# The weight block that the last product reads is cut last, and what was queued around it is reordered

## What is computed

```
uv = jax.nn.gelu(h @ w_in, approximate=False)          # stage 0: layer 0, gated mixer
u, v = jnp.split(uv, 2, axis=-1)
v = _rmsnorm(v, v_norm_g)
z = jnp.einsum("gts,bnsgc->bntgc", w_causal, v) + b_s.T[None, None, :, :, None]
y = (u * z) @ w_out
...
y = jnp.square(jax.nn.relu(h @ mlp_w_up[layer])) @ mlp_w_down[layer]   # stages 1 and 2: layers 0 and 1
```

## Time and profile before

| | |
|---|---|
| median of 3 runs | 2595.98 us (2595.35 to 2597.56) |
| the profiled execution's own time | 2595.35 us |
| span from its first to its last instruction | 2593.3 us |
| PE busy in the span | 2523.0 us (97%) |
| DVE busy | 1581.6 us (61%) |
| ACT busy | 988.1 us (38%) |
| mean granted clock of TensorE, of full speed | 0.991 |

### The profile page before, as it was taken

How to read it: one execution, slowest core, us unless ns; L and a number is a source line. 1 busy time by engine, 2 the same in 40 slices (tenths; PEclk the granted TensorE clock), 3 DMA queues, 4 the chain that set the end, 5 groups by cost and what they waited for, 6 DMA issues and landing times.

```text
span 2593.3 us, 33660 instructions
## 1 busy us (share of the span) xinstructions
PE 2523.0 (97%) x12220; PEld 2061.2 (79%) x12220; DVE 1581.6 (61%) x1907; ACT 988.1 (38%) x1423; POOL 149.0 (6%) x151
## 2 busy tenths in 40 slices
PE   6999999999999999999999997999999999999999
PEld 4888888888888878888898886666788888888887
DVE  6878766668867656675723624777258565544442
ACT  5543342236454421111302323777326445311110
POOL 0000000000000000000000003666000000000000
PEclk9999999999999999999999997999999999999999
DMA  6335573213444475553142353564322332632311
GB/s 253 126 134 182 192 265 106 98 57 146 166 151 151 174 276 176 204 186 114 51 157 91 113 173 99 114 137 105 123 114 94 110 117 109 251 122 82 112 47 68
DMA packets 122980, 359.60 MB, mean 139 GB/s; under 512 B 12032, under 2 KB 28416, under 8 KB 118912
## 3 DMA queue, kind: packets, MB, share of 16 engines
q1 hardware_dynamic: 122880, 358.23, 41.0%
HBM read 270.10 MB, written 88.08 MB: 138 GB/s over the span
## 4 chain that ended last, share of the span: by engine, by line
PE 84%; DVE 7%; DMA 3%; ACT 3%; issue 1%; SPq 0%; DVEq 0%; ACTq 0%
PE PS L2034 24%; PE PS L2036 24%; PE PS L2035 24%; DVE KEEP L1954 2%; DMA MODRAW<-in_modw 2%; PE PS L2514 2%; PE PS L2501 2%; PE PS L2482 1%; ACT PS L1269 1%; PE PS L2138 1%; PE PS L2140 1%; PE PS L2139 1%; PE PS L2438 1%; PE PS L2483 1%; DVE T_RAW L1553 1%
## 5 line engine op out<-in xcount | busy, mean ns | idle before, releaser
L2034 PE MATMUL PS<-HID_HI,W_HI 128*128 128x512 f32 x1024 | 400.1, 391 | 5.8 <-DVE HID_LO L1604 5.0
L2035 PE MATMUL PS<-HID_LO,W_HI 128*128 128x512 f32 x1024 | 398.5, 389 | 0.0
L2036 PE MATMUL PS<-HID_HI,W_LO 128*128 128x512 f32 x1024 | 398.5, 389 | 0.0
L374 ACT ACTIVATE W_HI<-RAW 128x1024 fp32r<-128x1024 f32 x114 | 119.5, 1059 | 615.5 <-PE PS L2036 510.2
L1450 DVE SCALAR_TENSOR_TENSOR X<-PS,MODV,X 128x1024 f32<-128x1024 f32 x124 | 159.0, 1282 | 284.2 <-PE PS L2036 275.6
L2034 PE MATMUL PS<-H_HI,W_HI 128*128 128x512 f32 x700 | 277.5, 396 | 3.7 <-DVE H_LO L1394 2.6
L2036 PE MATMUL PS<-H_HI,W_LO 128*128 128x512 f32 x700 | 273.5, 391 | 0.0
L2035 PE MATMUL PS<-H_LO,W_HI 128*128 128x512 f32 x700 | 273.3, 390 | 0.0
L2034 PEld LDWEIGHTS PS<-HID_HI,W_HI 128*128 128x128 f32 x1024 | 192.2, 188 | 50.4 <-DVE HID_LO L1604 7.9
L2036 PEld LDWEIGHTS PS<-HID_HI,W_LO 128*128 128x128 f32 x1024 | 192.2, 188 | 40.0
L2035 PEld LDWEIGHTS PS<-HID_LO,W_HI 128*128 128x128 f32 x1024 | 192.3, 188 | 39.5 <-issue 0.2
(11 more groups left out here) (223 smaller groups left out, 4922.7 us busy)
## 6 DMA issues: line engine op xcount, KB each, us to landing
RAW<-in_wt SPq DMA_DIRECT2D x208, 512.0 KB, 4.0
MODRAW<-in_modw SPq DMA_DIRECT2D x96, 512.0 KB, 3.5
HRAW<-hid_scratch SPq DMA_DIRECT2D x14, 2048.0 KB, 9.5
hid_scratch<-TN SPq DMA_DIRECT2D x90, 256.0 KB, 2.2
hid_scratch<-SCR SPq DMA_DIRECT2D x84, 256.0 KB, 2.2
x_scratch<-X SPq DMA_DIRECT2D x3, 4096.0 KB, 13.9
X<-x_scratch SPq DMA_DIRECT2D x6, 2048.0 KB, 9.0
QK<-qk_scratch SPq DMA_DIRECT2D x16, 768.0 KB, 6.3
```

The source lines that it names most:

```text
L374: act.activation(ring_view(W_HI, n), raw_view(n), ACT.Copy).then_inc(sem["w_hi"], 1)
L2034: pe.matmul(dst, w_hi, m_hi, start=first, stop=False)
L2035: pe.matmul(dst, w_hi, m_lo, start=False, stop=False)
L2036: return pe.matmul(dst, w_lo, m_hi, start=False, stop=last)
```

## The change

A22 becomes the last block that is cut, on ACT and on DVE, in every pair; since `load_pair` still waits for it, the load of the next pair's weights moves behind it too. In SP's queue `load_pair` now stands behind `store(p, 0, 0, 0, 0)` and one or two `load_mod`. `first_pair` begins with `c11`, and cuts the five blocks behind `c21`; in pair 1 (`second`) `c11` stands first. `WS_RAW` moves from the place of MODRAW to the place of WY_HI and WY_LO and is loaded after the last product of pair 12. TensorE's program is not edited.

```diff
--- before.py
+++ after.py
@@ -29,7 +29,7 @@
 PAIRS = UPS // 2 - 2
 PRODUCTS = 7
 BLOCKS = 6
-A1, A22, S2, S1, S3, S4 = range(BLOCKS)
+A1, S2, S1, S3, S4, A22 = range(BLOCKS)
 RELU_AT = {2: 1, 5: 2, 6: 3, 7: 4}
 VPAIRS = 6
 VHALF = [0, 1, 1, 0]
@@ -287,7 +287,7 @@
 
         V_TOT = at("V_TOT", [P, 2, HALF], F32, RX + 28 * KB)
         V_IN = at("V_IN", [P, 2, 2, HALF], F32, RX + 16 * KB)
-        WS_RAW = at("WS_RAW", [P, GROUPS, CHUNK], F32, RC)
+        WS_RAW = at("WS_RAW", [P, GROUPS, CHUNK], F32, RX + 24 * KB)
         W_RAW1 = at("W_RAW1", [P, 8, RING * P], F32, RR)
         R_RAW0 = at("R_RAW0", [P, 4, HALF], F32, RB)
         PO2 = at("PO2", [P, 2, HALF], F32, RB + 48 * KB)
@@ -535,10 +535,10 @@
                         sp.dma_start(RAW[:, f, :], wt[(p * 2 + t0 + 6 + f).v]).then_inc(sem[f"raw_in{f}"], 16)
 
                 def pair(p, x):
-                    load_pair(p + 1)
                     store(p, 0, 0, 0, 0)
                     if mods:
                         load_mod(sp, p // 2 * 3 + GMODS + 1 + 2 * x)
+                    load_pair(p + 1)
                     if mods and x == 0:
                         load_mod(sp, p // 2 * 3 + GMODS + 2)
                     store(p, 2, 0, 1, 1)
@@ -616,22 +616,22 @@
                     store(p, None, 1, 3, 1)
 
                 def v_pair(p):
-                    load_pair(p + 1)
                     store(p, 0, 0, 0, 0)
                     load_mod(sp, p + 1)
+                    load_pair(p + 1)
                     stores(p)
 
                 def u_pair(p, mods):
                     first = p * 3 + VPAIRS - 3 * VPAIRS
-                    load_pair(p + 1)
                     store(p, 0, 0, 0, 0)
                     for n in range(1, min(mods, 2) + 1):
                         load_mod(sp, first + n)
+                    load_pair(p + 1)
                     store(p, 2, 0, 1, 1)
                     store(p, 3, 1, 2, 0)
-                    store(p, None, 1, 3, 1)
                     if mods > 2:
                         load_mod(sp, first + 3)
+                    store(p, None, 1, 3, 1)
 
                 def load_v(u):
                     g, half = group_of(u), u % 4 // 2
@@ -654,10 +654,8 @@
                 u_pair(Count(PAIRS - 3), 2)
 
                 p = Count(PAIRS - 2)
-                sp.wait_ge(sem["mod_red"], GMODS)
-                sp.dma_start(WS_RAW[:], spw).then_inc(sem["spw_in"], 16)
+                store(p, 0, 0, 0, 0)
                 load_pair(p + 1)
-                store(p, 0, 0, 0, 0)
                 sp.wait_ge(sem["product"], count_of(0, p, PRODUCTS, 6).v)
                 for b in range(2):
                     sp.wait_ge(sem[f"pl_out{b}"], 64)
@@ -665,6 +663,8 @@
                 load_v(0)
                 load_v(1)
                 store(p, 2, 0, 1, 1)
+                sp.wait_ge(sem["product"], count_of(0, p, PRODUCTS, 7).v)
+                sp.dma_start(WS_RAW[:], spw).then_inc(sem["spw_in"], 16)
                 store(p, 3, 1, 2, 0)
                 store(p, None, 1, 3, 1)
 
@@ -1102,9 +1102,8 @@
                 plain(1)
                 act.wait_ge(sem["x_spilled"], 16 + 32 * h0)
                 block_cut(Count(0), 0, A1)
-                block_cut(Count(0), 0, A22)
                 plain(2)
-                for b in (S2, S1, S3, S4):
+                for b in (S2, S1, S3, S4, A22):
                     block_cut(Count(0), 0, b)
                 t_cut(1, 3)
                 t_cut(2, 5)
@@ -1618,13 +1616,16 @@
                         cut_lo(dve, Count(t0 + UPS + 2))
                         c21(p, x)
                         return
+                    second = p.i is None and p.c == 1
+                    if second:
+                        c11(p, x)
                     block_cut(p + 1, 1 - x, A1)
                     weight_sums(p + 1, 1 - x)
-                    block_cut(p + 1, 1 - x, A22)
                     if kind in ("v", "u0"):
                         for e in range(2, 4):
                             add_v(p - 1, e)
-                    c11(p, x)
+                    if not second:
+                        c11(p, x)
                     if mods:
                         mod_reduce(dve, p // 2 * 3 + GMODS + 2 * x)
                     elif kind == "v":
@@ -1644,6 +1645,7 @@
                     elif kind in ("u0", "u"):
                         mod_reduce(dve, p * 3 - 2 * VPAIRS + 1)
                     block_cut(p + 1, 1 - x, S4)
+                    block_cut(p + 1, 1 - x, A22)
                     if kind == "v":
                         add_v(p, 1)
                     c12(p, x)
@@ -1680,16 +1682,14 @@
 
                 def first_pair():
                     p = Count(0)
+                    c11(p, 0)
                     block_cut(p + 1, 1, A1)
                     weight_sums(p + 1, 1)
-                    block_cut(p + 1, 1, A22)
-                    c11(p, 0)
-                    for b in (S2, S1, S3):
-                        block_cut(p + 1, 1, b)
                     c22(p, 0)
-                    block_cut(p + 1, 1, S4)
                     c12(p, 0)
                     c21(p, 0)
+                    for b in (S2, S1, S3, S4, A22):
+                        block_cut(p + 1, 1, b)
                     if mods:
                         mod_reduce(dve, p // 2 * 3 + GMODS)
                         mod_reduce(dve, p // 2 * 3 + GMODS + 1)
@@ -1725,6 +1724,7 @@
                 t_cut(3, 3)
                 block_cut(Count(0), 0, S3)
                 block_cut(Count(0), 0, S4)
+                block_cut(Count(0), 0, A22)
                 t_cut(4, 4)
                 first_pair()
                 pair(Count(1), 1)
```

## The result

The changed kernel takes 2613.73 us (median of 4 runs, 2609.2 to 2614.82), beside 2595.66 us for the kernel before in the same series: 1.0065 times as long, 95% interval 1.0048 to 1.0083. It is slower by 18 us. The profiled execution took 2611.83 us, 2609.8 of it in the span. Run again later (e12) it was 1.0074 times the kernel before (1.0057 to 1.0090).

What follows compares the result with a forecast made beforehand. TensorE, busy 2523.0 of 2593.3 us, was taken as the bound; +1.4 (stage 0) − 0.65 + 0.4 (stage 1) − 0.65 (stage 2) made +0.5 us, so 2596.5 us, range 2594.0 to 2600.5.

Steps and rivals of the forecast that it cites:

- Steady pairs with one reduction: First loop: RAW issued 9.0 us later, landing still hidden with 0.8 us to spare; cost 0.
- Pairs with three reductions: Stage 0, pairs 6 to 11: cycle through RAW's load 18.5 us, under TensorE's 19.04; cost 0, margin 0.5.
- The rival: Load becomes the loop: RAW's landing sets the cycle in stage 0's pairs; about 2603 us, chance 0.12.
- Pair 12 and V_IN, "3 us spare": load_v goes from 337.14 to about 339; the scaling that needs it has 3 us until TensorE turns it.
- Spatial weights, hidden with 0.9 us: Loaded after pair 12's seventh product, masked by 346.7 to 348.1; ScalarE takes them at 348.99, so hidden.
- The lock rival: Weights landing after 347.7 make GpSimd's mask collide with VectorE's cut: +2.2 us in all, 2598.2; chance 0.07.
- First pair, stage 0, 1.4 us: Later RAW makes c21 of pair 1 late; TensorE's third product of pair 2 goes on at 135.2: 1.4 us lost.
- c11 first: Pair 0's seventh product no longer waits for VectorE's addition: gain 0.65 us each in stages 1 and 2, 0 in stage 0.
- Stage 1's late c21, 0.4: Pair 1's c21 ends at 681.3, TensorE wants it at 681.02: 0.4 us lost.
- Stage 2, 0: Nothing is reduced, RAW has no MODRAW ahead, and the walk is over 3 us shorter: 0 lost.

Runs made afterwards that it cites:

- e6: Kernel before with A22 cut last and SP's new queue order; spatial weights and VectorE's order in pairs 0 and 1 old: 2607.95 us, 1.0059.
- e5: Changed kernel with each MODRAW load issued in pairs 6 to 11 of stage 0 bringing 64 KB, not 512 KB: 2599.13 us, 1.0022.
- e11: Changed kernel with pair 12's load of RAW queued behind V_IN and the spatial weights: 2604.88 us, 1.0043 times the kernel before.
- e7: Kernel before (A22 second, RAW first in the queue) with the change's new first pair and late spatial weights: 2592.56 us, 0.9994.
- e10: Kernel before with only SP's new order, load_pair behind the first store and one or two MODRAW loads: 2595.31 us, 1.0005.
- e2: Changed kernel with RAW queued ahead of the second MODRAW load in pairs 6 to 11, A22 still last: 2621.52 us, 1.0101.
- e13: Changed kernel with the three later stores of pairs 6 to 10 queued behind the next MODRAW load: 2602.71 us, 1.0032.
- e9: Kernel before with idle work on VectorE ahead of c21 in pair 1 of each stage, making TensorE wait: 2602.39 us, one execution.
- e3: Changed kernel with VectorE's old order in pair 0 of each stage, A22 still cut last: 2614.61 us, 1.0084.
- e1: Changed kernel with the spatial weights back at their old place and loaded at the head of pair 12: 2605.26 us, 1.0048.

## Why the prediction was wrong

I forecast 2596.5 us, no difference, within 2594.0 to 2600.5; it is 2613.7. The range missed it by 13 us. Step by step:

- **Steady pairs with one reduction: right.** RAW is issued 9 us later and hidden; pairs 3 to 5 lose 0.0.
- **Pairs with three reductions, "cost 0, margin 0.5": the step that failed.** The sum was right in form; A22 to issue (0.86) and ScalarE (1.09) came as written. The landing was mis-sized: 4.7 was taken from the earlier trace rows, where two stores are ahead of RAW and nothing behind it, and it was 6.3 as a mean. The second reduction waited 0.55 us more for MODRAW, so that A1 to A22 took 12.45 for 11.8. Together 18.5 became 20.7, 20.7, 21.5, 19.0 and 21.0. A margin of 0.5 us in a closed chain was under the scatter of one of its terms; I gave that case 0.12, and priced it with 5.5 and 0.3 us a pair. The rival's mechanism is what e6 and e5 show.
- **Pair 12 and V_IN, "3 us spare": failed.** I moved the issue of load_v 2 us and left its landing alone. But the late A22 (349.75, for the chain above) puts 1 MB of RAW right ahead, and V_IN took 8.1 us for its first tile. In e11, without that 1 MB ahead, it took 5.0.
- **Spatial weights, hidden with 0.9 us: right alone, wrong in this change.** Landing 3.5 us and mask at 342.96 in e7, 9.2 us and 362.85 here. The wait behind it was for VectorE's H_LO, 3.58 us. The lock rival was not met: the mask ran when VectorE was idle.
- **First pair, stage 0, 1.4 us: mechanism right, size short.** The forecast end of c21 plus 0.14 was 135.2, and TensorE went on at 135.10. That the two times agree is luck: all of stage 0 ran 0.7 us earlier in this execution, and RAW landed in 5.3 us where 4.7 was taken. The wait cost 1.9 to 2.2, and 1.8 in one execution of two for the clock, a term that I had not in the sum at all. The Trainium skill's fit ("DMA: Bandwidth & Descriptors", section "Anatomy of one DMA — SWDGE (gpsimd) path"), from which I had estimated 4.4 us for this landing, was further off than the row.
- **c11 first: right,** 0.65 in stages 1 and 2, in all kernels that have it. **Stage 1's late c21, 0.4:** 1.1 to 1.3 us at product 2 of pair 2, and in one of the two executions 0.8 more a pair later. RAW landed in 4.6 us as taken. Late were, in the profile of the changed kernel, the first reduction (by 0.5 us) and the second, which waited 4.0 us for its MODRAW where 3.4 was taken and stood ahead of A1. **Stage 2, 0: right.**

Left open: why a landing behind the same transfers varies by 2 us within one execution, by what means stores behind a load slow it, why e10's landings are short all the same, and what decides whether the clock falls behind a wait of about 2 us. Whether the reduction could be moved behind the cut of A1, so that RAW may go ahead of MODRAW, was not tried.

## What to carry to other kernels

Before you let a single-buffered load wait for a later reader, write the chain from that reader round to itself as one sum, and compare it with the bound's cycle at the longest landing you have seen, with all transfers of that moment ahead and behind; a margin under the scatter of the landing is none. When one load moves in a queue, take every transfer behind it as later too, by the bytes now ahead of it. Price a wait of about 2 us on TensorE at up to twice its length.

## What the runs showed of the hardware

- A load of 2 x 512 KB lands its first tile in 3.3 us with no load just ahead (e2), and in 5.9 us as a mean of 42 (4.6 to 7.0) with 512 KB issued 1.2 us ahead and two 256 KB stores 1.3 and 2.1 us behind. With the stores 4 us behind it is 4.9 (4.3 to 5.8, five loads of e13); the stores without the 512 KB ahead leave it at 3.4 (e5).
- Behind waits of 1.79 (changed kernel), 2.56 (e6) and 2.86 us (e9) TensorE went on at 1.2 GHz for 1.7 to 1.8 us of extra time; behind waits of 1.50 and 1.55 (e9), 2.04 (e12) and 2.61 us (e3) it stayed at 2.4 GHz.
- GpSimd's mask of 128x1024 took 1.09 us beside an idle VectorE (e7) and 1.55 us in e1, where it ran across VectorE's sums.
